# Weight splitting in a three-layer forward pass on Trainium2: one pass per half against one pass per two-half tile

## What is computed

```python
proj = h @ w_in[l]
x = x + mixed @ w_out[l]
x = x + conv_ffn(rmsnorm(x, ffn_norm[l]), w_up[l], ffn_conv[l], ffn_conv_bias[l], w_down[l])
```

## Time and profile before

| | |
|---|---|
| median of 3 runs | 2113.77 us |
| profiled execution | 2112.93 us, span 2110.9 us |
| TensorE matmul busy | 2095.0 us (99%) |
| weight loads | 1828.3 us (87%) |
| VectorE | 1619.3 us (77%) |
| ScalarE | 1327.2 us (63%) |
| granted TensorE clock | 0.999 |
| weight loads by DMA | 377.34 MB in the queue of SyncE, 54.2% of 16 engines |

### The profile page before, as it was taken

How to read it: one execution, slowest core, us unless ns; L and a number is a source line. 1 busy time by engine, 2 the same in 40 slices (tenths; PEclk the granted TensorE clock), 3 DMA queues, 4 the chain that set the end, 5 groups by cost and what they waited for, 6 DMA issues and landing times.

```text
span 2110.9 us, 34665 instructions
## 1 busy us (share of the span) xinstructions
PE 2095.0 (99%) x13468; PEld 1828.3 (87%) x13468; DVE 1619.3 (77%) x2958; ACT 1327.2 (63%) x2626; POOL 13.5 (1%) x26
## 2 busy tenths in 40 slices
PE   9999999999999999999999999999999999999998
PEld 8878888888888888888888888888888888988887
DVE  7899766787788888666888867777686777689874
ACT  7866457775676666545666666555566655567764
POOL 0000000000000000000000000000000000000000
PEclk9999999999999999999999999999999999999999
DMA  8544434665465555555555555555555555654464
GB/s 281 177 147 146 164 117 148 225 217 188 160 199 192 195 193 193 196 190 197 193 193 195 191 193 196 195 187 194 188 187 179 170 194 192 189 166 159 152 208 139
DMA packets 107811, 389.86 MB, mean 185 GB/s; under 512 B 12368, under 2 KB 12624, under 8 KB 106880
## 3 DMA queue, kind: packets, MB, share of 16 engines
q1 hardware_dynamic: 105264, 377.34, 54.2%
q0 software_dynamic: 2096, 10.00, 1.3%
q10 hardware_dynamic: 288, 0.32, 0.0%
HBM read 384.36 MB, written 2.13 MB: 183 GB/s over the span
## 4 chain that ended last, share of the span: by engine, by line
PE 90%; DVE 7%; ACT 2%; issue 1%; DMA 0%; SPq 0%; DVEq 0%; ACTq 0%
PE main L604 84%; PE two L604 4%; DVE W L1107 2%; PE two L607 1%; DVE gt L1107 1%; DVE PPw L1107 0%; DVE GV L1113 0%; DVE AQ L1107 0%; ACT W L1817 0%; ACT L1816 0%; DMA RAW<-ws 0%; DVE GK L1113 0%; DVE PB L1107 0%; ACT PPw L1817 0%; DVE GQ L1113 0%
## 5 line engine op out<-in xcount | busy, mean ns | idle before, releaser
L1817 ACT ACTIVATE W<-RAW 128x512 fp32r<-128x512 f32 x1416 | 877.0, 627 | 599.1 <-PE main L604 593.1
L604 PE MATMUL main<-A,W 128*128 128x256 f32 (+2 forms) x7200 | 1248.5, 333 | 2.2 <-DVE W L1107 2.2
L1107 DVE TENSOR_TENSOR W<-RAW,W 128x512 fp32r<-128x512 f32 x1416 | 956.9, 686 | 354.0 <-ACT W L1817 345.5
L604 PEld LDWEIGHTS main<-A,W 128*128 128x128 f32 (+1 forms) x7200 | 1087.3, 187 | 154.5 <-issue 5.8
L604 PE MATMUL main<-H,W 128*128 128x512 f32 (+1 forms) x1408 | 239.7, 333 | 0.0
L604 PEld LDWEIGHTS main<-H,W 128*128 128x128 f32 x1408 | 212.2, 188 | 27.3
L604 PE MATMUL main<-B,W 128*128 128x512 f32 (+1 forms) x1216 | 197.0, 324 | 0.3 <-DVE B L1107 0.3
L604 PEld LDWEIGHTS main<-B,W 128*128 128x128 f32 x1216 | 176.4, 188 | 20.4 <-issue 0.5
L604 PE MATMUL main<-W,A 128*128 128x512 f32 (+1 forms) x672 | 150.2, 378 | 0.0
L604 PEld LDWEIGHTS main<-W,A 128*128 128x128 f32 x672 | 117.9, 188 | 22.4 <-issue 0.5
L604 PE MATMUL main<-W,B 128*128 128x512 f32 x384 | 88.5, 391 | 0.0
(11 more groups left out here) (329 smaller groups left out, 1370.3 us busy)
## 6 DMA issues: line engine op xcount, KB each, us to landing
RAW<-ws SPq DMA_DIRECT2D x707, 512.0 KB, 3.4
CB<-cscr POOLq DMA_DIRECT2D x4, 1024.0 KB, 5.4
XT<-xT POOLq DMA_DIRECT2D x4, 512.0 KB, 7.6
MS<-memT POOLq DMA_DIRECT2D x4, 512.0 KB, 11.2
xs<-xT SPq DMA_DIRECT2D x7, 256.0 KB, 7.5
out<-YT SPq DMA_DIRECT2D x7, 256.0 KB, 2.5
CST<-cst SPq DMA_DIRECT2D x1, 1272.0 KB, 7.9
G<-g POOLq DMA_DIRECT2D x1, 1024.0 KB, 5.9
```

What stands on the lines that cost most here:

```text
L604: return e.matmul(o, l, r, start=start, stop=True, skip_group_check=True)
L1107: return e.tensor_tensor(o, a, b, op)
L1817: return e.activation(o, i, f, bias=bias, scale=scale, accum_out=accum)
```

## The change

Instead of one hi and one lo per half there is one hi and one lo per tile, from half SINGLES = 6 on and outside of the small halves. The tile operation reads the 1024 columns of a RAW tile and writes both neighbouring slots j % 6 and j % 6 + 1 (j even) through one access pattern. It waits for both slots, signals both halves at once, and is issued at the even half's step. The odd half's call does nothing. HI_AHEAD goes from 5 to 4, LO_AHEAD from 4 to 3.

```diff
-NRAW, NW, HI_AHEAD, LO_AHEAD = 5, 6, 5, 4
+NRAW, NW, HI_AHEAD, LO_AHEAD = 5, 6, 4, 3
+SINGLES = 6
+        def tile_written(j, lo):
+            slots_ = W.rearrange("p (n x) -> p n x", x=PITCH)[:, j % NW:j % NW + 2]
+            if form_of(*HALVES[j][0:2]) != "wide":
+                o = whole_spots(j)[lo]
+                return slots_[:, :, o:o + 512]
+            a, b = pair_spots(j)[lo]
+            o, gap = min(a, b), abs(a - b)
+            v = slots_[:, :, o:o + 2 * gap].rearrange("p n (t x) -> p n t x", t=2)[:, :, :, 0:256]
+            return v if a < b else v[:, :, ::-1]
+        def by_tile(j):
+            return j >= SINGLES and HALVES[j][0] not in MINI
             def lo(j):
-                if j < NH:
+                if j >= NH or by_tile(j) and j % 2:
+                    return
+                if by_tile(j):
+                    w.wait_ge(s_hi, j + 2)
+                    tt(tile_written(j, 1), tile_loaded(j), tile_written(j, 0).bitcast(F), ALU.subtract).then_inc(s_lo, 2)
+                else:
                     w.wait_ge(s_hi, j + 1)
                     tt(written(j, 1), loaded(j), written(j, 0).bitcast(F), ALU.subtract).then_inc(s_lo, 1)
             def hi(j):
+                if j >= NH or by_tile(j) and j % 2:
+                    return
...
+                if by_tile(j):
+                    w.wait_ge(s_mm, j - NW + 2)
+                    copy(tile_written(j, 0), tile_loaded(j)).then_inc(s_hi, 2)
+                else:
                     if j >= NW:
                         w.wait_ge(s_mm, j - NW + 1)
                     copy(written(j, 0), loaded(j)).then_inc(s_hi, 1)
```

More of the change, by code:

```diff
@@ L397, in written, with tile_loaded @@
             return v if a < b else v[:, ::-1]
+        def tile_written(j, lo):
[7 more added lines that the diff above has]
+            return v if a < b else v[:, :, ::-1]
+        def tile_loaded(j):
+            x = RAW[:, j // 2 % NRAW, :]
+            if form_of(*HALVES[j][0:2]) != "wide":
+                return x.rearrange("p (n x) -> p n x", n=2)
+            return x.rearrange("p (n t x) -> p n t x", n=2, t=2)
+        def by_tile(j):
+            return j >= SINGLES and HALVES[j][0] not in MINI
         def loaded(j):
@@ L1822, in hi @@
             def hi(j):
[L1823 to L1827, removed]
+                if j >= NH or by_tile(j) and j % 2:
+                    return
+                if j:
+                    w.wait_ge(s_raw[j // 2 % NRAW], 16 * (j // 2 // NRAW + 1))
+                else:
+                    w.wait_ge(s_rawf, 16)
+                if by_tile(j):
+                    w.wait_ge(s_mm, j - NW + 2)
+                    copy(tile_written(j, 0), tile_loaded(j)).then_inc(s_hi, 2)
+                else:
                     if j >= NW:
```

## The result

The changed kernel takes 2133.61 us (median of 4 runs, 2132.42 to 2134.76) against 2113.84 us: **19.8 us slower**, ratio 1.009 with a 95% interval of 1.0078 to 1.0102. The forecast of 2114.8 us and the range up to 2121.5 us were both missed.

A forecast was written before the change was run, and what follows sets the result against it. TensorE was taken as 90% of the chain, with VectorE's list the bound from 80 to 187 and 1850 to 1900 us. -2.8 + 3.8 = +1.0 us on the 2113.77 median gave 2114.8 us, range over all 2108.5 to 2121.5.

The forecast's parts named there:

- The quiet stretch: Where TensorE's weight stream alone is the chain: the even half's lead falls from 5.4 to 3.1 us, costing 0 us.
- the prices of the operations: Tile operations taken as 1024-column ones: 1.04 us on ScalarE, 1.22 on VectorE; upper end 1.26 and 1.38.
- rival C: The tile operation costs two singles (1.26, 1.38 us), nothing is saved: 2118.6 us, chance 0.08.
- the loads: SyncE's loads wait at most 0.95 us longer for the tile's lo, with 13.6 us of room: 0 us.
- the start: First six halves stay single; the tile of halves 6 and 7 is ready just ahead of TensorE: 0 us, bounds 0 and 0.5.
- the five places: Near 100, 455, 1651, 1885 and 2004 us TensorE waits for a late even half: +3.8 us, 6.0 with nothing hidden.
- some 100: Sign that the forecast is right: VectorE busy some 100 us less.
- Rival A: Slower: the lead becomes the bound in crowded stretches, at even halves whose odd half had under 2.3 us; 2122.3 us, chance 0.20.
- its 2 us near 134 us: Rival A's addition at halves 82 and 83: some 2 us more if not hidden by TensorE's 1.84 us wait for another operand.
- the even half becomes ready when the odd one was, plus 0 (full VectorE queue) to 0.95 us: Where queues are behind, the tile stands at the odd half's old place; it costs where the odd half's lead was short.
- What is queued behind it on ScalarE isn't held longer by TensorE: Work behind the tile's hi waits no longer for TensorE; the copy holds it 0.43 us longer in even steps, 0.52 less in odd.
- The -2.8 us: Gain from fewer passes: 1.7 us from 80 to 187 us, 0.8 from 1850 to 1900, some 0.3 near 1650; at most about -7.

The follow-up runs named there:

- the pairs: The changed kernel with each tile operation broken into two singles at the same places behind the same joint waits, against the kernel before: 2134.03 against 2114.73 us, +19.3.

## Why the prediction was wrong

**What held.** The quiet stretch, where the lead of 3.1 us was enough; the prices of the operations (rival C falls); the loads and the start (half 6 was 0.3 us later, inside its bounds of 0 and 0.5); that the even half of a tile whose odd half had little lead is where TensorE would stand, and the five places found by it. VectorE's busy time fell by 62.7 us and not by some 100. Rival A named the right direction and part of the mechanism, the late even half, at a chance of 0.20 and a size of 8.5 us; it had no joint wait in it, and its 2 us near 134 us didn't come (half 82 ends 2.1 us later than before, half 83 makes up 2.2). The rule cited beside it, that breaking up instructions of engines which aren't saturated but cause bubbles may help (the Trainium skill, Perfetto Trace Analysis, Optimizing Scalar/DVE Operations), names the right sign; but the pairs show that it wasn't the instruction that had to be broken up. With broken instructions and joint waits the loss stays, +19.3 us; with the waits apart too, it is 6.7.

**The step that failed first** is "the even half becomes ready when the odd one was, plus 0 (full VectorE queue) to 0.95 us". It took the odd half's time from the old trace as if the two lists ahead of it still ran as before. They don't. VectorE now waits at a tile for two high parts where it waited for one, and what stands behind it waits too; where ScalarE's next piece needs something from behind VectorE's pass, the 0.5 us comes back each round. The five places, taken at 3.8 us with 6.0 as the most, measured, as growth of the delay over the halves around them: 2.6 near 100 us, 1.4 near 455, 2.2 near 1651, 2.7 near 1885 (0.7 of it at half 1272, just ahead of the place) and 3.8 from 2004 to 2038 us, 12.7 us in all.

**The second** is that only places with a short lead in the old trace were counted. Halves 221, 813 and 1151 had over 4 us of it in the trace of before, and none of the three stalls is for weights. They are the loop's (with two steps between copy and subtraction, LO_AHEAD 2, they go or shrink), and a loop is found by following who waits for whom round two engines and not by the lead. "What is queued behind it on ScalarE isn't held longer by TensorE" looked at the waits for TensorE alone; it missed the wait of VectorE for ScalarE.

**The third** is the gain. The -2.8 us assumed that where the chain runs through VectorE, less work there shortens it. From 80 us on to the same half as at 187 us the stretch took 110.5 us, in place of 107: VectorE's busy time against that of before

```profile
80.00:190.50 110.50, 103.21 (x928) 86.85 (x927) 98.20 (x163) 71.37 (x111) 1.53 (x2) 1.00 0.45 146
...
80.00:187.00 107.00, 102.50 (x924) 86.56 (x922) 99.03 (x190) 74.84 (x140) 1.53 (x2) 1.00 0.46 150
```

went down by 0.8 us (99.03 to 98.20; columns are TensorE, weight loads, VectorE, ScalarE), and its idle time up by 4.3 (107 - 99.0 = 8.0, 110.5 - 98.2 = 12.3). The chain through VectorE was a chain through its waits as well; the one wait of 2.42 us near 100 us is 3.52 now:

```profile
101.50 1.22 DVE L1128 TENSOR_TENSOR W<-RAW,W 128x1024 fp32r<-128x1024 f32 x1 [3.52 <-ACT W L1843]
```

**What adds up.** Moving the places 3.1 us, two passes in a row 3.6 (6.7 - 3.1), the joint slot wait 2.2, VectorE's joint wait for the high parts 10.4, joining the instructions 0.5: 19.8 us. Only the 10.4 us is a difference of two runs whose intervals stand clear of each other; the intervals behind 3.6, 2.2 and 0.5 overlap, and the 3.1 us has 1.3 to 5.3. How much of the 10.4 us is the loop proper and how much the late even half at crowded places isn't settled: halves 221, 813 and 1151 add up to some 3.4 us in the changed kernel, from 2004 to 2038 us both act together, and the kernel with only the subtraction by tile shows that most of such a loss can come without the loop.

## What to carry to other kernels

When work of one producer-consumer pair is joined into larger units, count what the joint signal makes the consumer wait for, and not only how long the joined instruction is: here the joint waits were 12.6 of the 19.8 us, the instruction's length hardly any. Where two engines hand work to each other both ways, in order, compute the round trip with the joined units in it (here 3.07 us) and hold it against what the bounding engine needs for the same work (2.72 us); both engines can be idle part of the time and still be the bound. And an engine that is busy 93% of a stretch (99 of 107 us) isn't relieved by less work there, if the work is moved behind one of its waits.

## What the runs showed that wasn't expected

A cut of 701 instructions and 62.7 us of busy time on VectorE (1619.3 to 1556.6), and of 115.5 us on ScalarE, came with a longer kernel. And distances in the lists are worth more than the passes: LO_AHEAD 3 with single passes costs 2.4 us, LO_AHEAD 2 with tile passes 31.8, 12 us more than LO_AHEAD 3 with the same passes.
